# Projection stage of a hybrid RWKV-7 / RG-LRU layer: stores, sigmoids, square root and weight split at other places of an item's slot

## What is computed

```python
rw_l, xb_l, gb_l, gt_l = split_columns(u_lat @ lp['w_in'])     # the projection
# for each direction d, on the RWKV columns after a mix of neighbouring tokens:
kk = kk / jnp.maximum(jnp.sqrt(jnp.sum(kk * kk, axis=-1, keepdims=True)), 1e-12)
w = -jax.nn.softplus(-(lp['w0'][d] + f['wd'] @ lp['w2'][d])) - 0.5
decay = jnp.exp(-jnp.exp(w.astype(jnp.float32)))
a = jax.nn.sigmoid(lp['a0'][d] + f['ad'] @ lp['a2'][d])
k = f['k'] * (1.0 + (a - 1.0) * lp['k_a'])
bonus = jnp.sum(f['r'] * k_sum * lp['r_k'], axis=-1, keepdims=True) * f['v']
```

## Time and profile before

| | us |
|---|---|
| median of three runs | 4840.54 (4838.01 to 4842.72) |
| the profiled execution | 4835.96 |
| its span, first to last instruction | 4833.8 |
| the projection stage, PE's first to last matmul | 145.8 to 1332.4 |
| busy over the span: PE / DVE / ACT / POOL | 3702.3 / 2335.1 / 1650.1 / 938.6 |
| mean granted TensorE clock over the span | 0.895 |

### The profile page before, as it was taken

The page is one execution under the profiler, slowest core; times in us unless marked ns, Lnnn a source line. Parts: engine busy times, 40 slices in busy tenths (PEclk is TensorE's granted clock), DMA queues, the critical chain, the costliest instruction groups (busy, mean ns, idle before and its releaser), DMA issues. The chain is left out here.

```text
span 4833.8 us, 121632 instructions
## 1 busy us (share of the span) xinstructions
PE 3702.3 (77%) x53101; PEld 3252.6 (67%) x53101; DVE 2335.1 (48%) x3847; ACT 1650.1 (34%) x2441; POOL 938.6 (19%) x828
## 2 busy tenths in 40 slices
PE   4887778889922167777777776989739999999993
PEld 2766666667811057777767676977529999999993
DVE  4145555551078823333333334653476666666664
ACT  3245454542124212122222223433314444444444
POOL 2200000001000054345335420530000111110110
PEclk8898889999966579999999998999859999999996
DMA  4233333332210052333233313744226766766675
GB/s 155 79 115 136 126 132 126 132 122 94 68 60 29 27 147 55 88 78 91 69 91 78 74 30 121 242 130 154 82 70 193 213 198 208 213 202 203 212 212 197
DMA packets 562440, 610.36 MB, mean 126 GB/s; under 512 B 65618, under 2 KB 466836, under 8 KB 560404
## 3 DMA queue, kind: packets, MB, share of 16 engines
q1 hardware_dynamic: 515604, 492.25, 33.1%
q0 software_dynamic: 21856, 80.75, 5.8%
q10 hardware_dynamic: 24480, 29.72, 2.0%
HBM read 443.09 MB, written 159.40 MB: 125 GB/s over the span
## 5 line engine op out<-in xcount | busy, mean ns | idle before, releaser
L647 PE MATMUL moe_h<-moe_xt_hi,moe_w_hi 128*128 128x256 f32 x2048 | 582.5, 284 | 16.4 <-DVE moe_xt_lo L526 14.8
L526 DVE TENSOR_TENSOR moe_w_lo<-moe_w_lo_whole,moe_w_hi 128x2048 fp32r<-128x2048 f32 (+1 forms) x258 | 453.5, 1758 | 264.7 <-ACT moe_w_hi L704 188.8
L647 PE MATMUL moe_h<-moe_xt_lo,moe_w_hi 128*128 128x256 f32 x2048 | 580.6, 283 | 0.0
L647 PE MATMUL moe_h<-moe_xt_hi,moe_w_lo 128*128 128x256 f32 x2048 | 580.5, 283 | 0.0
L1962 PE MATMUL inward_pp<-u_u_hi,inward_w_hi 128*128 128x512 f32 (+1 forms) x1360 | 547.0, 402 | 19.7 <-POOL inward_w_lo L2118 19.7
L1962 PE MATMUL inward_pp<-u_u_lo,inward_w_hi 128*128 128x512 f32 (+1 forms) x1360 | 531.0, 390 | 0.0
L1962 PE MATMUL inward_pp<-u_u_hi,inward_w_lo 128*128 128x512 f32 (+1 forms) x1360 | 528.8, 389 | 0.0
L647 PEld LDWEIGHTS moe_h<-moe_xt_hi,moe_w_hi 128*128 128x128 f32 x2048 | 393.6, 192 | 29.0 <-issue 25.2
L647 PEld LDWEIGHTS moe_h<-moe_xt_lo,moe_w_hi 128*128 128x128 f32 x2048 | 393.8, 192 | 3.7
L647 PEld LDWEIGHTS moe_h<-moe_xt_hi,moe_w_lo 128*128 128x128 f32 x2048 | 393.7, 192 | 0.0
L1962 PEld LDWEIGHTS inward_pp<-u_u_hi,inward_w_hi 128*128 128x128 f32 x1360 | 268.4, 197 | 83.8 <-POOL inward_w_lo L2118 19.9
(11 more groups left out here) (371 smaller groups left out, 9636.6 us busy)
## 6 DMA issues: line engine op xcount, KB each, us to landing
moe_w_lo_whole<-in_moe_w SPq DMA_DIRECT2D x387, 512.0 KB, 4.8
scratch_ops<-inward_ops SPq DMA_DIRECT2D x72, 514.0 KB, 3.8
scan_over<-scratch_ops SPq DMA_DIRECT2D x72, 512.0 KB, 10.3
inward_w_lo_whole<-in_w_in SPq DMA_DIRECT2D x38, 512.0 KB, 4.4
scan_aq<-scratch_ops SPq DMA_DIRECT2D x36, 516.0 KB, 5.3
scratch_gates<-inward_out SPq DMA_DIRECT2D x64, 256.0 KB, 2.1
all_late<-in_w_mod POOLq DMA_DIRECT2D x16, 1024.0 KB, 8.7
rest_modsum<-scratch_gates SPq DMA_DIRECT2D x64, 256.0 KB, 4.1
```

Source lines behind the costliest of these rows:

```text
L526: return nc.vector.tensor_tensor(x_lo, x, x_hi.bitcast(F32), ALU.subtract)
L647: mm = nc.tensor.matmul(hb[ft % 2][m][:, 0:CAP], w_, x, start=(k == 0 and part == 0), stop=(k == KD - 1 and part == 2))
```

## The change

Five calls move; no instruction's work is changed. On SP, `store_ops(s)` goes from phase 1 to phase 0, and `store_bonus(s)` from phase 2 to phase 1, behind `store_values(s+1)`. On ACT, `rates(s+1)` goes from phase 1 to phase 0, behind `load(s+2)` and ahead of `evict`; `roots(s+1)` and `keep(s+2)` go from phase 1 to phase 2; and `upper` for a tile is done one unit later, behind the eviction of the first unit after the tile's last.

```diff
                 s, phase = slot_of(k)
-                if phase == 1 and -1 <= s < NI:
-                    if s >= 0:
-                        store_ops(s)
+                if phase == 0 and 0 <= s < NI:
+                    store_ops(s)
+                elif phase == 1 and -1 <= s < NI:
                     if s + 1 < NI:
                         store_values(s + 1)
-                elif phase == 2 and 0 <= s < NI:
-                    store_bonus(s)
+                    if s >= 0:
+                        store_bonus(s)
...
                     if s + 1 < NI:
                         square(s + 1)
                         load(s + 2)
-                elif phase == 1 and -1 <= s < NI:
+                        rates(s + 1)
+                elif phase == 2 and -1 <= s < NI:
                     if s + 1 < NI:
-                        rates(s + 1)
                         roots(s + 1)
                         keep(s + 2)
                 if k:
                     evict(k - 1)
-                    if k - 1 in ends:
-                        upper(ends[k - 1] + 2)
+                    if k - 2 in ends:
+                        upper(ends[k - 2] + 2)
```

## The result

| | us |
|---|---|
| changed kernel, median of four runs | 4624.66 (4618.77 to 4629.65) |
| kernel before, median of four runs | 4841.44 (4838.01 to 4842.72) |
| ratio | 0.9553, 95% interval 0.9536 to 0.9569 |
| profiled execution of the changed kernel, its span | 4625.64, 4622.8 |

The change takes 216 us, 4.5%, off the kernel; 4622 us had been forecast. What follows was measured on several chips of the same kind, and the medians of the kernel before lie 15 us apart on them (4829.89 to 4844.65). So all comparisons go by the ratio to the kernel before on the same chip, and us are that ratio times 4841.44. The intervals of the ratios are 8 us to either side, 13 for the bonus store alone.

The account below looks back on a forecast made before the run. A chain of waits through stores, DVE and ACT was taken to hold PE at 23.6 us a slot. Saving 219.0 in the stretch and 4.4 at the head, less 5, gives 218.4 us: median 4622, range 4610 to 4680.

Parts of the forecast that it names:

- PE's pace as the floor: Item stretch: PE without waits takes 18.52 us per slot of long units, 15.93 with one short unit, against 23.6.
- The 5 us set aside for what remains: Item stretch: 5 us given back in all for the remaining loop where lengthenings meet, in at most 4 slots.
- The head: First item: the later weight rounding clears the way for the first load, where PE stood 6.24 us; 4.4 us counted.
- Operand stores: SP, issued one unit earlier: ACT waits 0 to 2 us; cost 0, at most 1 us in short slots.
- PE does not notice: Operand stores: PE needs the square at T + 12, T being the last-but-one unit's end; ACT has it about T + 4.
- Bonus store: SP, issued one unit earlier: bonus sum ready at T + 5 to T + 6; PE's 104.8 us of waits go.
- Sigmoids, root and copies: ACT: sigmoids ahead of phase 0's eviction delay it 3 to 4 us, covered by four banks; root and copies cost 0.
- rival D: Slower: SP's operand stores wait for step "Q", delaying output and phase-1 stores; 26.3 us a slot, 4938 us; chance 0.02.
- Rounding: ACT, weight rounding one unit later: its transfer has landed, so waits of about 4.8 us go; cost 0.
- The loop that is left: Bonus store, DVE and ACT to the next eviction: 12.0 us, plus 2.8 behind a weight load and 2.2 beside POOL's split.
- Rival B: Stores still release PE late in 16 slots, 1 us stopped plus 3.5 us at lower clock: 44 us, 4665; chance 0.14.
- Rival C: Another serial chain keeps slots at 20.82 us, only the rounding's wait gone: saves 100 us, 4740; chance 0.08.

## Why the prediction was right, step by step

**PE's pace as the floor.** The two slots of the earlier trace rows gave 15.93 and 18.52 us, and every slot of the changed kernel from slot 0 to slot 33 takes one or the other to within 0.05. The item stretch was forecast to shrink by 219.0 us. From slot 0 to slot 34 it went from 805.7 to 596.2 us, 209.5 for 34 slots, and the whole stage from 1332.0 to 1112.3, 219.7 with the head. The 5 us set aside for what remains were 0: in these slots PE never waits.

**The head** was mis-sized. 4.4 us were forecast and 0.8 came; PE's first item matmul came 1.5 us earlier, and slot 0 began 0.8 us earlier. The step that failed is "it clears the way for the first load": ACT was free at 247.1, but its first load was issued at 249.91, because in the code that load also waits until the stores of the first tiles, the last of them that of unit 19, have landed.

**Outside the stage** nothing was forecast. In the profiled executions the rest of the program took 3501.8 us before and 3510.5 after, 8.7 us against the gain. It need not be an effect of the change: two kernels with moves undone, profiled on one chip, took 3501.9 us (rounding back) and 3511.4 us (ACT's moves back) for the same code.

**How near the figure came** is partly luck. The stage was forecast to gain 218.4 us and gained 219.7, with the head 3.6 us too large and the remainder 5 us too large, which cancel. The profiled execution took 4625.64 us where 4617.6 were forecast, 8.0 us more; the median, forecast 4.6 us above it, lay 1.0 us below. So the 2.7 us by which the median of 4624.66 missed 4622 are less than the errors behind it.

**Operand stores.** Expected 0 to 2 us of wait; measured eight waits of 1.7 us at the most. The transfer was mis-sized: behind a weight load it takes 6.7 to 8.2 us from issue to release, not 4.6 to 4.8. Undone, the move costs 31 us, which the step "PE does not notice" would have called nothing: it held for the wait of 4.75 us, not for 8.4.

**Bonus store.** Its step was right and the most important, worth 158 us when undone. Forecast as "the 104.8 us of PE's wait go", it was under-sized. It left out the 49.1 us for the square, and a stop of PE also costs clock: of the 209.5 us gained from slot 0 to slot 34, 148 are PE's idle time and 62 are the same work at a higher clock. The forecast escaped this because its sum was made from PE's pace, not from the waits.

**Sigmoids, root and copies.** "Cost 0" holds in the changed kernel, where they gain 16 us; the root still waits for its floor there, 17.2 us in four slots. It does not hold without the bonus store. The prediction costed them only together; rival D, with the right engine but the wrong store, comes nearest to what the run of these moves alone showed: 59 us.

**Rounding.** "The waits of about 4.8 us go" was three quarters true (178.6 to 43.9 us), since ACT sometimes comes before the transfer has landed. It is worth 26 us alone, and with the others nothing that the times show (5 us of the stage in the profile).

**The loop that is left.** Worked out as 12.0 us, 17.0 with all lengthenings; measured 18.2 in the hardest slot. The 1.1 us over the sum lie on SP: from the eviction to the issue of the bonus store were 3.0 us (507.68 to 510.67) where 1.9 had been counted, since the weight load is issued in between and the value stores behind it took 1.21. The other terms held. From its issue to DVE's release (515.57) the bonus store took 4.9 us, the 2.1 + 2.8 of the sum, and 6.6 from the weight load's issue at 508.99 (4.9 in the earlier trace rows, where no value stores stood between). POOL's split stretched one DVE step from 0.68 to 2.88, the 2.2 us of the earlier trace rows. But such a stretch was expected in some 24 slots and came in eight. The step that fell short is that a stretch only makes the loop longer: it can also fall on the bonus sum that PE waits for, and with the items one unit later it did, and PE stopped.

**Rival B** needed PE to stop in some slots; it does not in the changed kernel. Its price per stop was also high: its 3.5 us at the lower clock had no row beside it, and where stops did come back, with the operand stores back at phase 1, PE's work took 607.06 us in place of 596 for ten stops, 1.1 us each and not 1.75. **Rival C** assumed that slots of 20.8 us were to be had by the rounding alone; 23.0 were measured.

## What to carry to other kernels

When engines are half idle and the bottleneck waits, write the waits down as one loop through all engines and queues, with the store that frees each buffer and what it is issued behind: here 176 us of waits cost 5 us at the most, while removing one of 105 on the engine that sets the time was worth 132 alone and 158 beside the other moves. Edits in such a loop do not add up (made alone they came to 26 + 33 + 132 - 59 = 132 us, each of these known to 8 to 13 us, together to 216), so one that is slower alone may be right with another. Take the floor from a stretch of the same trace in which the bottleneck never waits; it held here to 0.05 us a slot.

## What the runs showed of the hardware that was not expected

The slowdown of a DVE instruction beside a POOL split is not limited to copies. A product of two 128x512 operands, 0.68 us elsewhere, took 2.88 (517.12 to 520.00) while POOL's instruction ran from 516.91 for 2.54 us:

```profile
516.91 2.54 POOL L2118 TENSOR_TENSOR inward_w_lo<-inward_w_lo_whole,inward_w_hi 128x1024 fp32r<-128x1024 f32 x1 [24.22 <-ACT inward_w_hi L2075]
```

The Trainium skill ("SBUF — State Buffer", "SBUF: two separate sides") has this for VectorE instructions with two operands in SBUF against GpSimd instructions that read SBUF, and the rows agree: the product ended 0.55 us behind POOL's end at 519.45, as if it had run only then. Instructions without two operands in SBUF kept their length in the same profile: a reciprocal begun at 491.98, during a split from 490.29 to 492.69, took its usual 1.75 us, and a product with one operand in PSUM at 711.59, during a split from 710.57 to 713.08, its usual 0.42.

Two operand stores of 514 KB that had a 512 KB load ahead of them in the same queue released ACT 7.5 us after their issue (344.04 to 351.55, operand stores back), against 4.4 us where nothing stood ahead (547.29, the issue behind the earlier trace rows, to 551.65). Busy time by stretch for these two times, the first in the kernel with the operand stores back, the second in the kernel before:

```profile
344.00:351.60 7.60, 7.60 (x43) 6.18 (x42) 1.76 (x4) 0.05 (x1) 0.00 (x0) 1.00 0.90 295
547.30:551.70 4.40, 4.40 (x22) 3.39 (x20) 2.11 (x4) 0.05 (x1) 0.00 (x0) 1.00 0.92 355
```

The DMA engines are 0.90 and 0.92 busy there, though their mean over long stretches is only 0.38 to 0.53. The mean share hides that each store fills them while it runs. No run tells whether the store waits for its turn in the queue or shares full engines with the load, since none puts the load on another queue. In either case what is issued shortly ahead of a store that frees a buffer is a cost, to be written down with its length.
